# Eight gated experts on one core: one low part of the weights taken before the last low part of the activations, and the first trip through the expert pairs written out instead of looped

## The reference, cut to what matters

```python
logits = (xt @ w_router).astype(jnp.float32)
top_vals, top_idx = lax.top_k(logits, TOP_K)              # TOP_K = 2
top_w = jax.nn.softmax(top_vals, axis=-1)
combine = jnp.sum(jax.nn.one_hot(top_idx, N_EXPERTS, ...) * top_w[..., None], axis=1)
y = jnp.zeros_like(xt)
for e in range(N_EXPERTS):                                # N_EXPERTS = 8
    y = y + combine[:, e:e + 1] * swiglu(xt, w_gate[e], w_up[e], w_down[e])
```

## Time and profile before

| what | value |
|---|---|
| median of 3 runs | 2236.05 us (2235.39 to 2236.56) |
| the profiled execution | 2237.64 us, with a span of 2235.8 us |
| TensorE matmul busy | 2177.8 us, 97% of the span |
| VectorE busy | 1701.4 us, 76% |
| ScalarE busy | 1296.9 us, 58% |
| first matmul of the first expert to the end of the span | 1235.70 to 2235.8 us |
| the chain that ended last: TensorE's share | 88% |

### The profile page before, as it was taken

The page is one execution under the profiler, slowest core; times in us unless marked ns, Lnnn a source line. Parts: engine busy times, 40 slices in busy tenths (PEclk is TensorE's granted clock), DMA queues, the critical chain, the costliest instruction groups (busy, mean ns, idle before and its releaser), DMA issues.

```text
span 2235.8 us, 34057 instructions
## 1 busy us (share of the span) xinstructions
PE 2177.8 (97%) x13595; PEld 1946.5 (87%) x13595; DVE 1701.4 (76%) x1889; ACT 1296.9 (58%) x1291; POOL 75.9 (3%) x159
## 2 busy tenths in 40 slices
PE   7999999999999999999999999999999999999997
PEld 5998988999989999999899888888888888888886
DVE  6768967884786455558745888888888889888887
ACT  3564535663425444443434777777777777777775
POOL 5002200000000000000000000000000000000000
PEclk8999999999999999999999999999999999999999
DMA  9746858656535366555435799999999999999994
GB/s 281 190 139 203 267 185 228 185 178 183 176 104 182 100 169 185 175 151 172 141 109 193 277 366 359 368 332 359 356 373 353 341 368 359 364 345 365 357 369 179
DMA packets 414600, 563.81 MB, mean 252 GB/s; under 512 B 17098, under 2 KB 268212, under 8 KB 414448
## 3 DMA queue, kind: packets, MB, share of 16 engines
q1 hardware_dynamic: 409680, 555.26, 73.7%
q0 software_dynamic: 4768, 6.36, 1.2%
HBM read 559.75 MB, written 1.84 MB: 251 GB/s over the span
## 4 chain that ended last, share of the span: by engine, by line
PE 88%; DVE 4%; ACT 2%; issue 1%; DVEq 0%; ACTq 0%
PE pair L1184 63%; PE misc L1184 13%; PE pair L1244 4%; PE misc L1737 1%; DVE wlo L2179 1%; DVE wlo L1828 1%; PE pair L1705 1%; PE misc L1285 1%; PE misc L1264 0%; ACT whi L678 0%; DVE opl L1847 0%; PE misc L1417 0%; PE misc L1714 0%; PE misc L1715 0%; PE misc L1445 0%
## 5 line engine op out<-in xcount | busy, mean ns | idle before, releaser
L2179 DVE TENSOR_TENSOR wlo<-raw,whi 128x2048 fp32r<-128x2048 f32 x336 | 764.2, 2289 | 117.0 <-ACT whi L1066 116.0
L1066 ACT CAST whi<-raw 128x2048 fp32r<-128x2048 f32 x336 | 643.0, 1916 | 202.6 <-PE pair L1184 121.0
L1828 DVE TENSOR_TENSOR wlo<-raw,whi 128x2048 fp32r<-128x2048 f32 (+2 forms) x158 | 348.4, 2208 | 171.9 <-ACT whi L678 171.3
L1184 PE MATMUL pair<-hh,whi 128*128 128x256 f32 x1408 | 406.6, 289 | 5.6 <-DVE hl L1864 3.0
L1184 PE MATMUL pair<-hl,whi 128*128 128x256 f32 x1408 | 402.3, 286 | 0.0
L1184 PE MATMUL pair<-hh,wlo 128*128 128x256 f32 x1408 | 401.9, 285 | 0.0
L1184 PE MATMUL pair<-whi,oph 128*128 128x512 f32 x896 | 352.8, 394 | 4.2 <-DVE wlo L2179 4.2
L1184 PE MATMUL pair<-wlo,oph 128*128 128x512 f32 x896 | 349.3, 390 | 0.0
L1184 PE MATMUL pair<-whi,opl 128*128 128x512 f32 x896 | 349.2, 390 | 0.0
L678 ACT CAST whi<-raw 128x2048 fp32r<-128x2048 f32 (+2 forms) x158 | 290.1, 1836 | 88.1 <-PE pair L1184 74.5
L1184 PE MATMUL pair<-oph,whi 128*128 128x256 f32 x976 | 280.2, 287 | 5.2 <-issue 3.0
(11 more groups left out here) (465 smaller groups left out, 2777.9 us busy)
## 6 DMA issues: line engine op xcount, KB each, us to landing
raw<-in_moe_w_gate_dram SPq DMA_DIRECT2D x112, 1024.0 KB, 7.4
raw<-in_moe_w_up_dram SPq DMA_DIRECT2D x112, 1024.0 KB, 7.5
raw<-in_moe_w_down_dram SPq DMA_DIRECT2D x112, 1024.0 KB, 6.9
raw<-in_w_in_dram SPq DMA_DIRECT2D x38, 1024.0 KB, 6.4
raw<-in_w_mod_dram SPq DMA_DIRECT2D x24, 1024.0 KB, 5.7
raw<-in_w_up_dram SPq DMA_DIRECT2D x44, 512.0 KB, 5.2
raw<-in_w_xkv_dram SPq DMA_DIRECT2D x16, 1024.0 KB, 5.7
raw<-in_ffn_w_gate_dram SPq DMA_DIRECT2D x22, 512.0 KB, 4.0
```

Source lines behind the costliest of these rows:

```text
L1066: act.copy(whi[:, q, :], raw[:, r, :]).then_inc(sem("hi_ready"), 1)
L1184: ins = pe.matmul(out_, lhs, rhs, start=start and i == 0, stop=stop and i == 2)
L1828: dve.tensor_tensor(wlo[:, i_ % SPLIT, 0:size], raw[:, raw_of(n), 0:size], whi[:, i_ % SPLIT, 0:size].bitcast(F32), ALU.subtract).then_inc ...
L2179: dve.tensor_tensor(wlo[:, q, :], raw[:, r, :], whi[:, q, :].bitcast(F32), ALU.subtract).then_inc(sem("lo_ready"), 1)
```

## The change

Two things change.

First, VectorE makes the low part of slot 40 before the low part of the last activations: a call `upto(MOE_SLOTS - 2)` stands in front of `hidden_lo(JE - 1)`. It applies to every expert. The instructions are the same ones in another order.

Second, in pass 0 the loops over pairs on ScalarE, TensorE and VectorE, and the loop over experts on SyncE, become Python loops, so that their bodies are written out three (seven) times, with constants for what were registers. Pass 1 keeps its loops.

```diff
             def moe_pass(p):
-                with sp.Fori(0, NE - 1) as e:
+                def one(e):
                     for k in range(2, MOE_SLOTS):
                         load(e + NE * p, e, k)
                     for k in (0, 1):
                         load(e + NE * p, e + 1, k + MOE_SLOTS)
+
+                if p == 0:
+                    for e in range(NE - 1):
+                        one(e)
+                else:
+                    with sp.Fori(0, NE - 1) as e:
+                        one(e)
...
-                with act.Fori(0, NE // 2 - 1) as i:
-                    for u in range(2):
-                        moe_expert(i, u, p)
+                if p == 0:
+                    for i in range(NE // 2 - 1):
+                        for u in range(2):
+                            moe_expert(i, u, p)
+                else:
+                    with act.Fori(0, NE // 2 - 1) as i:
+                        for u in range(2):
+                            moe_expert(i, u, p)
...
                     if j in SCATTER_AT:
                         added(S, SCATTER_AT.index(j), misc[:, 1, :])
+                upto(MOE_SLOTS - 2)
                 hidden_lo(JE - 1)
```

More of the change, by code:

```diff
@@ L1793, in moe_pass @@
                 gather(NE // 2 * p, first=p == 0)
-                with pe.Fori(0, NE // 2 - 1) as i:
-                    for u in range(2):
-                        moe_expert(i, u, p)
+                if p == 0:
+                    for i in range(NE // 2 - 1):
+                        for u in range(2):
+                            moe_expert(i, u, p)
+                else:
+                    with pe.Fori(0, NE // 2 - 1) as i:
+                        for u in range(2):
+                            moe_expert(i, u, p)
                 for u in range(2):
@@ L2527, in moe_pass @@
                     zeroed(ye_lo).then_inc(sem("m_yl"), 1)
-                with dve.Fori(0, NE // 2 - 1) as i:
-                    for u in range(2):
-                        moe_expert(i, u, p)
+                if p == 0:
+                    for i in range(NE // 2 - 1):
+                        for u in range(2):
+                            moe_expert(i, u, p)
+                else:
+                    with dve.Fori(0, NE // 2 - 1) as i:
+                        for u in range(2):
+                            moe_expert(i, u, p)
                 for u in range(2):
```

## The result

The kernel after takes 2224.95 us (median of 7 runs, 2223.69 to 2229.50), where the kernel before takes 2236.05: 11.1 us less. The ratio is 0.995, with a 95% interval from 0.9939 to 0.9961. Forecast were 8.55 us less and 2227.5 us, with a range down to 2225.0. The direction and both mechanisms were as forecast.

A forecast was written before the change was run, and what follows sets the result against it. TensorE was taken to bound the expert section, so only its standstills could go: 4.0 + 0.8 + 4.65 - 0.9 = 8.55 us, from 2236.05 to 2227.5 us, range 2225.0 to 2232.4.

The forecast's parts named there:

- The moved low part: Before `down(6)` in four u=0 experts and the last: slot 40's low part going first saves 4.65 us, bounds 0 to 5.7.
- the 0.2 us left at each of the five places: Before `down(6)`: allowance of 0.2 us per place, as TensorE loads a matmul's weights one matmul ahead.
- The jumps: TensorE's two jumps back at pair ends: writing out the loop removes their gaps and slow restarts, 4.0 us, bounds 0 to 4.0.
- The table loads: ScalarE's activation table loads in the loop: five of six go, saving 0.8 us, bounds 0 to 1.02.
- The first expert's 0.8 us: Before slot 2 of the first expert: without one table load TensorE's late start there mostly goes, saving 0.8 us.
- hidden in any case: The four table loads behind the jumps: removing them gains nothing, as VectorE and ScalarE catch up within two slots.
- the rival in which the loop part gives nothing: Pair ends: gaps stay or written-out code costs what it saves; only the VectorE reordering counts, 2231.4 us, chance 0.07.
- The constants: Constants for registers in written-out experts: six experts may lose 0.15 us each, -0.9 us, bounds -0.9 and 0.
- The rival of starved straight code: Written-out pairs: late instruction fetches at 1.9 us each, seven giving 2240.8 us; chance of slower 0.08.
- nowhere: Written-out code: by the skill's page the straight copy would wait for instructions at no place, the same 4.0 us.

The follow-up runs named there:

- e2: Kernel before with all four engines' loops written out and VectorE's old order kept; 2230.21 us, ratio 0.9974 to the kernel before.
- e4: Kernel before with ScalarE's loop alone written out, old order kept; 2237.62 us, ratio 1.0001 to the kernel before.
- e3: Kernel before with TensorE's loop alone written out, old order kept; 2234.15 us, ratio 0.999 to the kernel before.
- e9: Kernel before with every load of expert weights cut to its first half; 998.9 us from the first expert on.
- e6: Kernel after with the low parts of slots 40 and 41 both before the last activations' low part; 2244.71 us, ratio 1.0047 to the kernel before.

## Why the prediction was wrong in size

**The moved low part** was forecast at 4.65 us and measures 6.0 among written-out kernels (`e2` to after). This is the term that was mis-sized, and the step that failed is the 0.2 us left at each of the five places, for an activations' low part that ends only 0.18 us ahead and for weights being loaded one matmul ahead. The end came nearly as computed (0.14 us ahead), the weight load shrank its lead from 0.22 to 0.09 us instead of delaying the matmul, and nothing was lost: that is 1.0 of the 1.35 us by which the term was too small. Most of the rest is that a looped place costs 1.2 us, not 1.11, once it is written out: its wait grows from 0.85 to 0.94 (`e2`).

**The jumps** were forecast at 4.0 us. The first profile agrees, with 3.79 us on the two u=1 experts by the earlier trace rows and the two restarts. But a single profile is one draw: in the second one the same u=1 experts are 2.83 and 1.79 us longer than the third trip's, and 2.7 more went into matmuls at the lower clock. I took one execution's gap for the price, and had no term for a clock that falls after a standstill, because the earlier trace rows shows none. The median will hold some of these executions, so what is removed is probably more than 4.0 us in the middle; how much, three profiles don't tell. The 6.3 us of `e2` against a forecast of 3.9 for its terms point the same way.

**The table loads.** One load of six stayed, as forecast. The first expert's 0.8 us was 0.77 in `e4`. But "hidden in any case" was wrong for the four behind the jumps. They were hidden by TensorE's gap, and `e3` shows their price when it goes: 1.5 us a trip. The sum was right only because both loops are written out together, and the rival in which the loop part gives nothing would have been close to true for TensorE's loop alone: from the first expert on `e3` takes 999.9 us against 1000.1, although its median is 2.4 us lower.

**The constants** were put at 0.15 us an expert. The u=1 experts in the middle take 124.31 to 124.40 us written out, and 124.21 to 124.33 in the third trip of a looping TensorE, so about 0.1. It comes in pieces of up to 0.07 us in several steps of an expert, whose cause stays open. With the three looped places whose wait grew by 0.09 the cost of writing out is 0.9 us, as forecast.

**The end of the program** had no term, since the code there is the same. It gave 0.8 us in the first profile, and 0.3 to 0.8 over all of them, by luck.

By the first profiles the sum is then 4.0 + 0.8 + 6.0 - 0.9 + 0.8 = 10.7 us, beside 10.7 measured from the first expert on and 11.1 in the medians. What the forecast of 8.55 lacked there is 1.35 us of the moved low part and 0.8 of the end. The rival of starved straight code is refuted: no wait named "issue" lies in the written-out experts, and the loads kept pace at a DMA share of up to 1.01. The rule of the Trainium skill (Runtime: NRT & Kernel Launch, "Instruction fetch mechanics") that a taken branch outside the window waits for a fetch is borne out here by `e9` and by the packets, with gaps from 0.77 to 3.27 us. Of a block's crossing in straight code the same section says that it is mostly hidden, which is less than the prediction's "nowhere". In the experts the trace agrees. The 0.95 to 1.53 us behind the jump at the program's end would be an exception if they are such a crossing, which no run here shows.

## What to carry to other kernels

A gap of the bounding engine hides the delays of the others at the same place; before costing them at nothing, ask whether the change also takes the gap away. A hardware loop whose body was entered again while the DMA queues were full cost the bounding engine a fetch of varying length here, and sometimes a stretch at the lower clock, so its price is a distribution and one profile is one draw of it. When an engine stands idle with its operands long made, look for a jump, and for a packet of the instruction queue, before believing the releaser that the profile names.

## What the runs showed of the hardware

- TensorE's granted clock fell to the 1.2 GHz level behind some standstills inside the experts, for 6 to 14 matmuls. It did so behind the six jump gaps from 1.99 to 3.27 us and behind four of the five waits of 2.66 us in `e6`, and not behind the four jump gaps from 1.53 to 1.87 us.
- The gap at a jump back of TensorE was 1.53 to 3.27 us with the DMA engines at a share near 1 and 0.77 to 1.12 us at 0.61. TensorE restarted 1.73 to 1.86 us after the end of an instruction packet in either case.
- Behind a jump forward over code that isn't run, VectorE stood still for 0.95 to 1.53 us between its last four additions in ten profiles, and 71 instructions that never run brought that gap back.
- A matmul whose weight load started 0.09 us ahead of it, where 0.22 is usual here, started on time.
- In this kernel ScalarE's table loads ran in every trip of the loop: six in three trips, and one when the body is written out.
